# Layer one's probabilities turned through DRAM instead of on TensorE, its value products in two banks, and the convolution's first tap on ScalarE

## What is computed

```python
proj = x @ w_in + b_in                       # 2048 -> conv value, conv glu, conv gate, q, k, v, attention gate
c_val, c_glu, c_gate, q, k, v, a_gate = split(proj)

# convolution branch: 1024 channels, 31 taps along the tokens, causal
h = c_val * sigmoid(c_glu)
h = conv_b + sum_k conv_w[k] * shift(h, 30 - k)       # depthwise
y_conv = silu(layer_norm_over_channels(h)) * silu(c_gate)

# attention branch: 16 heads of 64, 2 key/value heads, blocks of 128 tokens, window 128, a sink per head
scores = q . k * scale, masked                 # token block 0: 128 keys; token block 1: 256 keys
p = exp(scores - m);  denom = sum(p) + exp(sink - m)
y_attn = (p / denom) @ v * silu(a_gate)

x = layer_norm(alpha * x + concat(y_conv, y_attn) @ w_out + b_out)
```

## Time and profile before

| | us |
|---|---|
| median of three runs | 1613.49 |
| span of the profiled execution, first to last instruction | 1611.6 |
| TensorE busy | 1601.1 |
| VectorE busy | 1052.7 |
| ScalarE busy | 784.8 |
| GpSimd busy | 93.9 |

### The profile page before, as it was taken

How to read it: one execution, slowest core, us unless ns; L and a number is a source line. 1 busy time by engine, 2 the same in 40 slices (tenths; PEclk the granted TensorE clock), 3 DMA queues, 4 the chain that set the end, 5 groups by cost and what they waited for, 6 DMA issues and landing times.

```text
span 1611.6 us, 23663 instructions
## 1 busy us (share of the span) xinstructions
PE 1601.1 (99%) x8869; PEld 1361.1 (84%) x8869; DVE 1052.7 (65%) x1485; ACT 784.8 (49%) x1096; POOL 93.9 (6%) x155
## 2 busy tenths in 40 slices
PE   8999999999999999999999999999999999999999
PEld 8999889888877988788888888888888888888887
DVE  5989898878765767976666655555554555555544
ACT  4346664654544565664464644444443344444432
POOL 3000000000100000000000011111100001111100
PEclk9999999999999999999999999999999999999999
DMA  9555444858676553458654566666666556666663
GB/s 294 186 167 180 148 147 164 304 187 290 200 264 205 145 178 123 128 166 294 195 180 149 168 230 210 223 220 211 218 197 197 194 185 233 209 225 217 211 205 108
DMA packets 173403, 320.52 MB, mean 199 GB/s; under 512 B 7459, under 2 KB 43601, under 8 KB 172160
## 3 DMA queue, kind: packets, MB, share of 16 engines
q1 hardware_dynamic: 167184, 298.05, 56.5%
q0 software_dynamic: 6128, 21.23, 3.8%
HBM read 306.66 MB, written 12.58 MB: 198 GB/s over the span
## 4 chain that ended last, share of the span: by engine, by line
PE 98%; DMA 1%; issue 1%; POOL 0%; DVE 0%; ACT 0%; DVEq 0%; ACTq 0%; POOLq 0%
PE ps_g L385 26%; PE ps_g L387 26%; PE ps_g L386 26%; PE ps_g L430 4%; PE ps_g L431 4%; PE ps_g L432 4%; PE ps_m L308 1%; PE ps_m L1099 0%; PE ps_m L1157 0%; PE ps_m L955 0%; PE ps_m L1080 0%; POOL turned L879 0%; DMA hnT<-turned 0%; PE ps_g L405 0%; PE ps_g L404 0%
## 5 line engine op out<-in xcount | busy, mean ns | idle before, releaser
L461 DVE TENSOR_TENSOR lo<-raw,hi 128x1024 fp32r<-128x1024 f32 (+3 forms) x551 | 650.9, 1185 | 467.0 <-ACT hi L446 461.6
L446 ACT CAST hi<-raw 128x1024 fp32r<-128x1024 f32 (+3 forms) x551 | 561.7, 1021 | 725.7 <-PE ps_g L387 630.4
L385 PE MATMUL ps_g<-hi,aH 128*128 128x512 f32 (+3 forms) x1376 | 529.3, 385 | 0.0
L387 PE MATMUL ps_g<-hi,aL 128*128 128x512 f32 (+3 forms) x1376 | 519.9, 378 | 0.0
L386 PE MATMUL ps_g<-lo,aH 128*128 128x512 f32 (+3 forms) x1376 | 519.3, 377 | 0.0
L385 PEld LDWEIGHTS ps_g<-hi,aH 128*128 128x128 f32 x1376 | 258.8, 188 | 49.3 <-issue 3.6
L387 PEld LDWEIGHTS ps_g<-hi,aL 128*128 128x128 f32 x1376 | 258.6, 188 | 48.6
L386 PEld LDWEIGHTS ps_g<-lo,aH 128*128 128x128 f32 x1376 | 259.0, 188 | 45.9 <-issue 0.5
L430 PE MATMUL ps_g<-aH,hi 128*128 128x256 f32 x512 | 148.0, 289 | 1.2 <-DVE lo L455 1.2
L431 PE MATMUL ps_g<-aL,hi 128*128 128x256 f32 x512 | 145.9, 285 | 0.0
L432 PE MATMUL ps_g<-aH,lo 128*128 128x256 f32 x512 | 145.8, 285 | 0.0
(11 more groups left out here) (418 smaller groups left out, 1340.6 us busy)
## 6 DMA issues: line engine op xcount, KB each, us to landing
raw<-in_w_gu_dram SPq DMA_DIRECT2D x88, 1024.0 KB, 5.1
raw<-in_w_in_dram SPq DMA_DIRECT2D x60, 1024.0 KB, 5.0
raw<-in_w_down_dram SPq DMA_DIRECT2D x44, 1024.0 KB, 5.1
raw<-in_w_out_dram SPq DMA_DIRECT2D x32, 1024.0 KB, 5.1
raw<-in_w_in_dram SPq DMA_DIRECT2D x42, 512.0 KB, 5.0
raw<-in_w_ck_dram SPq DMA_DIRECT2D x8, 1024.0 KB, 5.4
raw<-in_w_cv_dram SPq DMA_DIRECT2D x8, 1024.0 KB, 5.5
turned<-hb POOLq DMA_DIRECT2D x88, 64.0 KB, 4.4
```

What stands on the lines that cost most here:

```text
L385: pe.matmul(dst, xh, wh, start=first, stop=False)
L387: last = pe.matmul(dst, xl, wh, start=False, stop=final)
L446: act.copy(step_view(hi, s), raw_view(s)).then_inc(s_hi, 1)
L461: dve.tensor_tensor(step_view(lo, s), raw_view(s), step_view(hi, s).bitcast(F32), ALU.subtract).then_inc(s_lo, 1)
```

## The change

Four edits belong together.

1. TensorE no longer transposes the probabilities and ScalarE no longer copies them. VectorE transposes 32x32 squares of both heads at once (`probs_blocks`, one 128x768 instruction per pair, slot +3), GpSimd stores them to DRAM with four transfers, waits for these, and loads the turned squares into `pT` with one.
2. The value products move from slots +5, +6 to +8, +9 and alternate between banks 2 and 3; `normalize` moves from +7 to +10.
3. The first tap and the bias are done on ScalarE (`first_tap`, 8 instructions in slots 9, 17, 49 and 57); 240 taps stay on VectorE, none of them in slots 32 to 39.
4. `GATE` goes from slots 67 and 74 to 68 and 77.

```diff
-        pT = put("pT", 190, [P, 2, 3 * P])
+        pT = put("pT", 190, [P, 2, 6, P])
+        sB = put("sB", 196, [P, 2, 6 * P])
+        turned1 = nc.dram_tensor("turned1", (2, 4, 32, 6, 4, 32), F32, kind="Internal").ap()
...
-        conv_units = 8 * TAPS
+        conv_units = 8 * (TAPS - 1)
...   (GpSimd)
+            for u in range(HEADS // 2):
+                pool.wait_ge(s_pb, u + 1)
+                if u >= 2:
+                    pool.wait_ge(s_pr, 16 * (u - 1))
+                for q in range(4):
+                    pool.dma_start(turned1[u % 2, :, :, :, q, :].rearrange("b r x c -> r x b c"),
+                                   sB[32 * q:32 * q + 32, u % 2].rearrange("r (x b c) -> r x b c", x=6, b=4)
+                                   ).then_inc(s_pw, 16)
+                pool.wait_ge(s_pw, 16 * 4 * (u + 1))
+                if u >= 2:
+                    pool.wait_ge(s_pv, 2 * u - 2)
+                pool.dma_start(pT[:, u % 2].rearrange("p x t -> p (x t)"),
+                               turned1[u % 2].rearrange("b r x q c -> (b r) (x q c)")).then_inc(s_pr, 16)
...
-        SM, EX, PT, PV, NM = 1, 2, 3, 5, 7
-        GATE = [G["ag1"]["s0"] + 3, G["ga0"]["s0"] + 2]
+        SM, EX, TB, PV, NM = 1, 2, 3, 8, 10
+        GATE = [G["ag1"]["s0"] + 4, G["ga0"]["s0"] + 5]
...   (TensorE: probs_T removed)
             def pv(u, h):
-                pe.wait_ge(s_pTc, n + 1)
-                if u >= 1:
-                    pe.wait_ge(s_yn, u)
+                pe.wait_ge(s_pr, 16 * (u + 1))
+                if u >= 2:
+                    pe.wait_ge(s_yn, u - 1)
...   (ScalarE: probs_copy removed)
+            def first_tap(j):
+                evacuated(act, G[f"cm{j}"])
+                act.wait_ge(s_pad, 1)
+                act.wait_ge(s_colsb, 2)
+                for ct in (2 * j, 2 * j + 1):
+                    act.activation(cT[:, ct, :], hT[:, ct, 0:T], ACT.Identity, scale=convw[:, ct, 0:1],
+                                   bias=cols[:, CB + ct:CB + ct + 1]).then_inc(s_tap0, 1)
...
+                        if p == G[f"cm{c}"]["s0"] + 9:
+                            first_tap(c)
...   (VectorE)
+            def probs_blocks(u):
+                b = 2 * (u % 2)
+                dve.wait_ge(s_exp, u + 1)
+                if u >= 2:
+                    dve.wait_ge(s_pw, 16 * 4 * (u - 1))
+                dve.transpose(sB[:, u % 2], sS[:, b:b + 2, :].rearrange("p h c -> p (h c)")).then_inc(s_pb, 1)
...
-                    rate = 1
+                    rate = 0
...
+                if p - TB in pair_slot:
+                    probs_blocks(pair_slot[p - TB])
```

More of the change, by code:

```diff
@@ L515, in stack_kernel @@
         s_conv = sem("conv_taps")
+        s_tap0 = sem("conv_first_tap")
         s_qt = sem("qk_transposed")
@@ L520, in stack_kernel @@
         s_exp = sem("exp_done")
-        s_pt = sem("probs_transposed")
-        s_pTc = sem("probs_T_ready")
+        s_pb = sem("probs_blocks_transposed")
+        s_pw = sem("probs_blocks_stored")
+        s_pr = sem("probs_T_loaded")
         s_pv = sem("pv_done")
@@ L947, in scores @@
                 last.then_inc(s_sc, 1)
[L949 to L956, removed]
             def pv(u, h):
-                n = 2 * u + h
-                pe.wait_ge(s_pTc, n + 1)
-                if u >= 1:
-                    pe.wait_ge(s_yn, u)
+                pe.wait_ge(s_pr, 16 * (u + 1))
+                if u >= 2:
+                    pe.wait_ge(s_yn, u - 1)
                 k = u // (HEADS // KVH // 2) * HD
-                o = (u % 2) * T + h * HD
-                pe.matmul(ps_m[3][:, o:o + HD], pT[:, h, 0:P], v_sb[:, 0, k:k + HD], start=True, stop=True)
+                bank, o = ps_m[2 + u % 2], h * HD
+                p0, p1, p2 = [pT[:, u % 2, 3 * h + j, :] for j in range(3)]
+                pe.matmul(bank[:, o:o + HD], p0, v_sb[:, 0, k:k + HD], start=True, stop=True)
                 o += P
-                pe.matmul(ps_m[3][:, o:o + HD], pT[:, h, P:2 * P], v_sb[:, 0, k:k + HD], start=True, stop=False)
-                pe.matmul(ps_m[3][:, o:o + HD], pT[:, h, 2 * P:], v_sb[:, 1, k:k + HD],
+                pe.matmul(bank[:, o:o + HD], p1, v_sb[:, 0, k:k + HD], start=True, stop=False)
+                pe.matmul(bank[:, o:o + HD], p2, v_sb[:, 1, k:k + HD],
                           start=False, stop=True).then_inc(s_pv, 1)
@@ L973, in attn_slot @@
                     scores(pair_slot[p])
-                for h in range(2):
-                    if p - PT - h in pair_slot:
-                        probs_T(pair_slot[p - PT - h], h)
                 for h in range(2):
@@ L1005, in before_y @@
                     pe.wait_ge(s_yat, 2)
-                    pe.wait_ge(s_pTc, HEADS)
             for g in groups[:11]:
@@ L1516, in exps @@
                 last.then_inc(s_exp, 1)
[L1518 to L1523, removed]
             def attn_slot(p):
-                for h in range(2):
-                    if p - PT - 1 - h in pair_slot:
-                        probs_copy(pair_slot[p - PT - 1 - h], h)
                 if p - EX in pair_slot:
@@ L2023, in conv_input @@
                                              ).then_inc(s_free[pair_of(g)], 1)
-            conv_order = [(j, k, c) for j in range(4) for k in range(TAPS) for c in range(2)]
+            conv_order = [(j, k, c) for j in range(4) for k in range(1, TAPS) for c in range(2)]
             conv_at = [0]
@@ L2034, in conv @@
                     ct = 2 * j + c
[L2035 to L2042, removed]
+                    if k == 1:
+                        dve.wait_ge(s_tap0, ct + 1)
+                        if c == 0:
+                            evacuated(dve, G[f"cm{j}"])
                     else:
                         dve.wait_ge(s_conv, i - 1)
-                        dve.scalar_tensor_tensor(out=cT[:, ct, :], in0=src, scalar=w, in1=cT[:, ct, :],
-                                                 op0=ALU.mult, op1=ALU.add).then_inc(s_conv, 1)
+                    dve.scalar_tensor_tensor(out=cT[:, ct, :], in0=hT[:, ct, k:k + T], scalar=convw[:, ct, k:k + 1],
+                                             in1=cT[:, ct, :], op0=ALU.mult, op1=ALU.add).then_inc(s_conv, 1)
             def softmax(u):
@@ L2054, in softmax @@
                 if u >= 2:
-                    dve.wait_ge(s_pt, 2 * u - 2)
+                    dve.wait_ge(s_pb, u - 1)
                 for h in range(2):
@@ L2070, in normalize @@
                 link(dve.reciprocal(rden[:, two, :], den[:, two, :]))
-                o = (u % 2) * T
                 dve.tensor_tensor(q_sb[:, :, 2 * u * HD:2 * (u + 1) * HD].rearrange("p t (h d) -> p t h d", h=2),
-                                  ps_m[3][:, o:o + T].rearrange("p (t h d) -> p t h d", t=TT, h=2),
+                                  ps_m[2 + u % 2][:, 0:T].rearrange("p (t h d) -> p t h d", t=TT, h=2),
                                   rden[:, two, :].rearrange("p h t -> p t h").unsqueeze(3).to_broadcast([P, TT, 2, HD]),
```

## The result

The changed kernel takes **1619.48 us** (median of 7 runs, 1617.67 to 1620.19); the kernel before, beside it on the same chip, 1613.35 (7 runs, 1613.03 to 1617.21). The ratio is 1.0029, with an interval of 1.002 to 1.0038: slower, by 0.3%. The forecast was 1617.2 in a range of 1612.5 to 1620. The profiled execution has a span of 1617.5 us, 5.9 more than 1611.6.

The account below looks back on a forecast made before the run. TensorE bounds the kernel, but a nearly full VectorE sets slot 83: 7.0 + 0.3 - 5.4 = 2.0 us, plus waits of 0.8 and 1.1, less some 0.2 slack, gives +3.7; 1613.49 + 3.7 = 1617.2 us, range 1612.5 to 1620.

Parts of the forecast that it names:

- VectorE is a second engine that is almost full.: From 181 to 269 us: VectorE is busy for 43.87 of 46 us, then 41.93 of 42.
- The transpose at 0.88 us: VectorE's new 128x768 transpose, one per pair: 0.88 us each, 7.0 us for eight, up to 7.4.
- Two waits remain: VectorE still waits for ScalarE's sigmoid at slot 56, about 0.8 us, and for its cast at slot 68, 1.1 us.
- +3.7 us at slot 83: Channel sums on TensorE, waiting for VectorE's last taps, start at 272.7 us instead of 269.0.
- TensorE gets there first: Ahead of slot 83 TensorE arrives at 271.5, 1.2 us before the taps, with waits of about 10 us in all.
- That is the whole possible gain: -6.5 us.: TensorE loses two groups of three transposes per pair, 0.48 and 0.33 us; 8 pairs make 6.5 us.
- The round trip is covered: Stores and load through DRAM take 14.4 us (bounds 13.0 and 16.8) of 17.1 us available in the last pair.
- GpSimd isn't held up: GpSimd's DMA issues in the pairs: VectorE's operations don't keep it from writing descriptors; 0.87 us per store issue.
- whatever moves slot 83 moves the end: After slot 83 TensorE has no wait over 0.5 us, so a shift there passes to the kernel's end.
- The rival with the clock: Waits on TensorE lower its granted clock; a few steps at half speed cost 2.9 us each; chance 0.03.
- no wait here is over 2 us: Argument against a lowered clock: none of TensorE's waits in the changed stage exceeds 2 us.
- the case that I thought likeliest: VectorE's taps set slot 83 later by 3.7 us; time 1617.2, own range 1616 to 1619; chance 0.60.

Follow-up runs that it names:

- light_after: Changed kernel with the first gate half's silu back in ScalarE's slot 66 and 40 convolution taps left out: 1609.21 us, ratio 0.9972 to the kernel before.
- light_before: Kernel before with 40 convolution taps left out, at 2 and 3 taps a slot: 1614.31 us, ratio 0.9999.
- silu_early: Changed kernel with the first gate half's silu back in ScalarE's slot 66, ahead of the last exponentials: 1617.29 us, ratio 1.002 to the kernel before.
- eight_stores: Changed kernel with the silu in slot 66 and each pair stored in eight transfers of 16 rows, not four of 32: 1618.03 us, ratio 1.0016.
- clock_split: Changed kernel with layer two's 32 short `cmp_scores` products cut into two halves one slot apart: 1617.85 us, ratio 1.0023 to the kernel before.
- before_split: Kernel before with layer two's 32 short `cmp_scores` products cut into two halves one slot apart: 1613.06 us, ratio 0.9994.

## Why the prediction was right, and where it missed

- *"VectorE is a second engine that is almost full."* Right, and the core of it. light_after against light_before is the test: the change with the silu early gains 3.9 us at slot 83 where VectorE has room, and loses 2.6 (silu_early) where it has none.
- *The transpose at 0.88 us.* 0.89 from start to start (143.73 to 144.62). All eight last 969 to 983 ns.
- *Two waits remain.* 0.8 us at slot 56, as forecast; 1.31 us at slot 68 for 1.1. Slot 68 opened at 223.05 where the working had 222.75.
- *+3.7 us at slot 83.* +4.0: the sums at 273.0 for 272.7. The parts hold singly as well: 1.4 us for the silu (silu_early), the rest for the transposes.
- *TensorE gets there first.* Its last product ahead of slot 83 ends at 272.1 where I had 271.5, and it waits 0.9 us for the taps, the last wait there, as the forecast asked. Its idle time from 143 to 273 us is 8.0 us (130 less 122.02 busy), where the working meant "about 10"; that working took 6.5 us of transposes off TensorE, and it was 4.9.
- *"That is the whole possible gain: -6.5 us."* Too large by a third. The 0.48 us of the chain is not what the group costs beside other small products (0.28, under light_after); eight pairs are worth 4.9 us. The +3.7 doesn't hang on this term, since VectorE sets slot 83, but whoever wants to know what the move could bring at best is misled by it.
- *The round trip is covered.* Right in the outcome, and its terms were not all right. Issues took 3.44 to 3.49 us for four (3.5 forecast), landing 4.0 (5.6), but the wait for the stores was 2.2 to 8.0 us where I had taken 5.3 for every pair. In the pair with 8.0 TensorE waited 2.1 us for the load, at 205.14, in time that VectorE's pace left over. eight_stores shows that a trip 1.5 us longer in the last pair still fits. The trip's lower bound of 13.0 doesn't come out of its own terms, 4 x 0.74 + 5.3 + 5.6 = 13.9; nothing rests on it.
- *GpSimd isn't held up.* Its 32 issues of stores took 866 to 902 ns each (0.87 forecast), with VectorE busy for 44.21 of 46 us. So the warning of the Trainium skill, "SBUF — State Buffer", section "SBUF: two separate sides", about VectorE's two-port modes does not bite with the operations that VectorE runs here.

**The term that was mis-sized** is what lies behind slot 83. The forecast said "whatever moves slot 83 moves the end", +3.7 for +3.7. It was +4.0 there and +5.9 at the end of the profiled execution, 1.6 of it a stretch at half clock in layer two. The rival with the clock had the right kind of mechanism and the wrong place: it looked at TensorE's waits in the pairs, with the argument "no wait here is over 2 us" (it was 3.4, and 6.7 in clock_split), where a low clock cost nothing in silu_early and some 0.5 us in clock_split, because VectorE sets the end of the stage or nearly so. The place that costs is behind 32 short products in layer two that the change doesn't touch. By their profiles and their spans, clock_split and before_split show that splitting those products takes these falls away in both kernels. Whether the changed kernel meets the fall more often than the kernel before, and why, is open: there are only seven runs of it, and nothing of the change touches that stretch except that it comes 4 us later. Comparing the lowest executions, about 1611.3 before and 1615.7 to 1616.0 after (whose mean clock of 0.999 says that they aren't free of falls), leaves 4.4 to 4.7 us, of which slot 83 explains 4.0.

In part the range did the work. The measured 1619.48 lies half a microsecond inside the upper end, 1620, and above the 1616 to 1619 of the case that I thought likeliest. That case is the one that the traces show, and its number was exceeded because four of the seven runs, by their spans and clocks, had a costly fall; the other three lie near 1617.7.

## What to carry to other kernels

Before work is moved off the bounding engine, find the synchronisation that both engines run into and ask how much idle time the receiving engine has ahead of it: here 5.4 us for 7.1 of transposes. Move only as many units as that time pays for; two or three of eight gained a microsecond at slot 83, all eight lost four. Read what the other engine gains from the starts of the instructions around the work and not from the durations of a chain: 4.9 us here and not 6.5. And a small operation that moves with the change (the silu) has to be followed on its own engine, since it cost a third of the loss by standing behind the wrong neighbour.

## What the hardware showed unexpectedly

- A half clock behind products that kept TensorE busy without a gap: 32 products of 3.48 us in all then seven products 0.43 us apart, 1.6 us lost; in some executions and not in others. In halves one slot apart (1.69 us for the second) it did not occur in 31 runs of three kernels, by their mean clock of 1.000 (the run of 4142.87 us not counted).
- The wait from the last of four GpSimd stores to the load's issue varied from 2.2 to 8.0 us in the changed kernel, beside a weight stream of 189 to 227 GB/s.
- Three transposes of 128x128 on TensorE cost 0.33 us when they stand alone between large products and 0.28 beside other small ones, though each group has a duration of about 0.5.
- ScalarE's table load took 1.28 us, and `Identity` for the first tap added none in these traces.
